# Memory attention and router of a hybrid decoder block: norms as numbers beside the products instead of rows ahead of them

## The reference, cut to what matters

```python
def rms_norm(x, g):                      # row by row, over the last axis
    return x * rsqrt(mean(x * x) + 1e-6) * g

# x: 256 tokens x 1024;  mem: 256 rows x 1024
x = x + parallel_head_groups(rms_norm(x, g_mix), ...)            # 16 heads, three kinds
q = rms_norm((rms_norm(x, g_xmem) @ w_mq).reshape(4 heads, 64), g_qm)
k, v = split(rms_norm(mem, g_mem) @ w_mkv);  k = rms_norm(k, g_km)
x = x + softmax(q @ k.T * 64 ** -0.5) @ v @ w_mo                 # memory attention
h = rms_norm(x, g_ffn)
logits = h @ w_router + b_router                                 # 32 experts, top 4
x = x + sum over experts of gate * (clamped_swiglu(h @ w_e1[e] + b_e1[e]) @ w_e2[e] + b_e2[e])
```

## Time and profile before

| | us |
|---|---|
| median of 3 runs | 1224.62 (1220.62 to 1225.78) |
| the profiled execution, its own time | 1226.69 |
| its span, first to last instruction | 1224.9 |
| TensorE busy | 1136.0 (93% of the span) |
| VectorE busy | 324.1 (26%) |
| ScalarE busy | 193.5 (16%) |
| GpSimd busy | 111.0 (9%) |
| mean granted TensorE clock | 0.965 of 2.4 GHz |

### The profile page before, as it was taken

The page is one execution under the profiler, slowest core; times in us unless marked ns, Lnnn a source line. Parts: engine busy times, 40 slices in busy tenths (PEclk is TensorE's granted clock), DMA queues, the critical chain, the costliest instruction groups (busy, mean ns, idle before and its releaser), DMA issues.

```text
span 1224.9 us, 13760 instructions
## 1 busy us (share of the span) xinstructions
PE 1136.0 (93%) x4992; PEld 459.6 (38%) x4992; DVE 324.1 (26%) x693; ACT 193.5 (16%) x391; POOL 111.0 (9%) x286
## 2 busy tenths in 40 slices
PE   6989978778999999999999999999999999999997
PEld 4656844653333333333333333333333333333332
DVE  4464644531121212111111112221111112111122
ACT  2133332211111111111111111111111111111111
POOL 1020100001001010000000000000111000001000
PEclk9979988677999999999999999999999999999999
DMA  7813335203999999999999999999999999999995
GB/s 259 319 35 138 134 102 194 102 1 135 403 430 429 429 429 429 428 429 429 428 428 428 428 428 428 428 428 428 428 430 429 428 429 430 430 428 429 428 429 238
DMA packets 44036, 430.54 MB, mean 351 GB/s; under 512 B 6289, under 2 KB 13713, under 8 KB 19185
## 3 DMA queue, kind: packets, MB, share of 16 engines
q1 hardware_dynamic: 43024, 427.67, 83.6%
q10 hardware_dynamic: 992, 2.62, 0.6%
HBM read 429.23 MB, written 1.05 MB: 351 GB/s over the span
## 4 chain that ended last, share of the span: by engine, by line
DMA 50%; PE 42%; DVE 4%; ACT 2%; issue 1%; SPq 0%; DVEq 0%; POOL 0%; ACTq 0%; POOLq 0%
DMA ring_w<-in_w_e_dram 49%; PE banks L580 12%; PE banks L267 11%; PE banks L561 8%; PE banks L593 3%; PE banks L255 2%; PE banks L509 1%; PE banks L302 1%; PE banks L536 1%; DMA w_in_cq<-in_w_in_dram 1%; PE banks L284 1%; PE banks L283 1%; PE banks L517 0%; PE banks L545 0%; DVE stat L1144 0%
## 5 line engine op out<-in xcount | busy, mean ns | idle before, releaser
L561 PE MATMUL banks<-ring,xg_T 128*64 128x512 f32 x2048 | 480.5, 601 | 27.2 <-DMA ring<-in_w_e_dram 25.3
L561 PEld LDWEIGHTS banks<-ring,xg_T 128*64 128x64 f32 x2048 | 134.3, 137 | 317.0 <-issue 239.8
L580 PE MATMUL banks<-ring_w,act_T 128*64 128x512 f32 x1024 | 237.8, 598 | 10.3 <-DMA ring_w<-in_w_e_dram 10.3
L1484 DVE TENSOR_TENSOR x_sb<-x_sb,banks 128x1024 f32<-128x1024 f32 x64 | 78.2, 1221 | 402.6 <-PE banks L536 386.0
L580 PEld LDWEIGHTS banks<-ring_w,act_T 128*64 128x64 f32 x1024 | 68.4, 136 | 150.7 <-issue 114.3
L1494 DVE TENSOR_TENSOR glu<-banks,b_T 128x512 f32<-128x512 f32 x32 | 22.1, 692 | 337.5 <-PE banks L593 337.5
L536 PE MATMUL banks<-y_sb,hot_gate_T 64*128 64x512 f32 x256 | 72.0, 640 | 1.7 <-ACT hot_gate_T L1071 1.7
L509 PE MATMUL banks<-h_sb,hot_slot 128*64 128x512 f32 x264 | 64.0, 607 | 2.5 <-POOL hot_slot L820 2.5
L1040 ACT COPY xg_rows<-banks 128x512 f32<-128x512 f32 x33 | 19.3, 586 | 294.0 <-PE banks L509 294.0
L1054 ACT COPY hidden<-banks 128x1024 f32<-128x1024 f32 x32 | 32.4, 1012 | 206.5 <-PE banks L561 206.5
L827 POOL COPY picked<-slot_table 128x2 f32 (+1 forms) x32 | 6.3, 196 | 579.2 <-PE banks L525 579.2
(11 more groups left out here) (257 smaller groups left out, 830.6 us busy)
## 6 DMA issues: line engine op xcount, KB each, us to landing
ring<-in_w_e_dram SPq DMA_DIRECT2D x128, 2048.0 KB, 23.8
ring_w<-in_w_e_dram SPq DMA_DIRECT2D x62, 2048.0 KB, 24.3
w_out_sb<-in_w_out_dram SPq DMA_DIRECT2D x1, 4096.0 KB, 13.4
ring_w<-in_w_e_dram SPq DMA_DIRECT2D x4, 1024.0 KB, 6.7
w_in_qk<-in_w_in_dram SPq DMA_DIRECT2D x1, 2048.0 KB, 14.3
w_mkv_sb<-in_w_mkv_dram SPq DMA_DIRECT2D x1, 2048.0 KB, 10.7
w_in_cq<-in_w_in_dram SPq DMA_DIRECT2D x1, 1536.0 KB, 11.7
w_in_qc<-in_w_in_dram SPq DMA_DIRECT2D x1, 1536.0 KB, 17.1
```

The source lines that it names most:

```text
L561: ins = TE.matmul(PS[SLOTS * h:SLOTS * h + SLOTS, B_W1 + b, :], left, ring1[:, u, 2 * F * j + F * h + 512 * b:2 * F * j + F * h + 512 * b ...
L580: ins = TE.matmul(PS[SLOTS * h:SLOTS * h + SLOTS, B_W2, :], actT[:, c % 4, c // 4, :], ring2[:, k, D * j + 512 * h:D * j + 512 * h + 512], ...
L1484: V.tensor_tensor(X[:, t, :], X[:, t, :], PS[:, first:first + 2, :].rearrange("p b n -> p (b n)"), ALU.add).then_inc(S("added"), 1)
```

## The change

It covers the stage between the last output projection and the first gather.

- Raw rows of `X` are transposed, not normalized ones. The gain vectors of the two norms are multiplied into the weights instead: `g_xmem` into `w_mq`, `g_ffn` into `w_router`, by GpSimd, from columns `gcol` that ScalarE's queue loads (2 x 1024 single numbers, in the place of the broadcast of `g_xmem`). `g_qm` and the score scale go into the gain of the memory keys.
- The scale of a row of x1 drops out of the normalized query but for the epsilon, which VectorE corrects (`shift`). The scale of a query and head goes into the exponential as its per-row factor; its square sum comes from TensorE (`query_sums`, with the two columns `halves`). The scale of a row of x2 (`y2`) is multiplied to the router's logits and into the one-hot tile of each gather; GpSimd multiplies `X` by the gain `g_ffn` for the gather's rows.
- Queries leave their product already transposed (`queries`: the weights are the stationary side), and values too (`mem_values`). Attention goes by tile instead of by head; the probabilities are normalized before they are transposed.
- The order of all engines in the stage is new. The first one-hot tile is made by VectorE, directly from the ranks. Gates, counts, gate transposes and tables come later, beside or behind the first gather; `give_biases` follows chunks 0 and 2 of the first step instead of standing ahead of chunk 0 and behind chunk 1.

```diff
+        def turn_x(name, added_name, t):
+
             for half in range(2):
-                merge("wd", t, half, range(5, KC))
-
-        pe.wait_ge(S("w_mq_in"), 16)
-        for t in range(NT):
-            pe.wait_ge(S("x1_rows"), t + 1)
-            turn_rows("x1_", H, t)
-            pe.wait_ge(S("turned_out"), turn.n)
-            multiply(f"q{t}", rows(t), lambda c: wmq[:, c, :], KC)
-        for t in range(NT):
-            pe.wait_ge(S("mem_q_normed"), t + 1)
-            turn_blocks(f"q{t}", [qm[:, t, P * j:P * j + P] for j in range(2)])
-        pe.wait_ge(S("turned_out"), turn.n)
-        for what, h in order(MEM_H):
-            {"score": score, "turn": turn_p, "value": value}[what](f"x{h}")
-        pe.wait_ge(S("mem_attended"), 1)
-        turn_blocks("om", [om[:, t, P * j:P * j + P] for j in range(2) for t in range(NT)])
-        pe.wait_ge(S("turned_out"), turn.n)
-        pe.wait_ge(S("w_mo_in"), 16)
-        for t in range(NT):
+                pe.wait_ge(S("mm_out"), left_no[f"{added_name}{t}{half}"])
+                turn_blocks(f"{name}{t}{half}", [X[:, t, P * c:P * c + P] for c in range(4 * half, 4 * half + 4)])
...
+        def queries(t):
+
+            bank = into(f"q{t}", [("q_left", t + 1)])
+            for j in range(2):
+                for c in range(KC):
+                    if j == 0 and c % 4 == 0:
+                        pe.wait_ge(S("turned_out"), turned_no[f"x1_{t}{c // 4}"])
+                    ins = TE.matmul(bank[:, P * j:P * j + P], wmq[:, c, P * j:P * j + P], hT[:, c, t * P:(t + 1) * P],
+                                    start=(c == 0), stop=(c == KC - 1))
+            ins.then_inc(S("mm_done"), 1)
...
+            pe.wait_ge(S("q_squared"), t + 1)
+            bank = into(f"ss{t}")
+            for j in range(2):
+                ins = TE.matmul(bank[:, j:4:2], qsq[:, j, t * P:(t + 1) * P], halves, start=True, stop=True)
...
+            pe.wait_ge(S("q_left"), t + 1)
+            banks = [into(f"s{par}{t}", [("mem_exped", 4 * t + 2 * par + 2)]) for par in range(2)]
+            for j in range(2):
+                for par in range(2):
+                    r = 64 * par
+                    ins = TE.matmul(banks[par][:, T * j:T * j + T], qmT[r:r + 64, j, t * P:(t + 1) * P],
+                                    memT[r:r + 64, j, :], start=True, stop=True)
...
+                pe.wait_ge(S("probs_normed"), 2 * t + par + 1)
+                turn_blocks(f"pm{t}{par}", [Pm[:, t, 512 * par + P * k:512 * par + P * k + P] for k in range(4)])
...
+            bank = into(f"o{t}")
+            for j in range(2):
+                for c in range(2):
+                    for par in range(2):
+                        a = 256 + 64 * (2 * j + par)
+                        b = 512 * par + 256 * j + P * c
+                        ins = TE.matmul(bank[64 * par:64 * par + 64, P * j:P * j + P], KVm[:, c, a:a + 64],
+                                        H[:, t, b:b + P], start=(c == 0), stop=(c == 1))
...
+        out_d(0, 0)
+        out_d(0, 1)
+        out_d(1, 0)
+        turn_x("x1_", "wd", 0)
+        out_d(1, 1)
+        pe.wait_ge(S("w_mq_scaled"), 1)
+        queries(0)
+        turn_x("x1_", "wd", 1)
+        query_sums(0)
+        mem_scores(0)
+        queries(1)
+        turn_probs(0)
+        query_sums(1)
+        mem_scores(1)
+        pe.wait_ge(S("w_mo_in"), 16)
+        mem_values(0)
+        mem_out(0)
+        turn_probs(1)
+        mem_values(1)
+        turn_x("x2_", "mo", 0)
+        mem_out(1)
+        pe.wait_ge(S("router_scaled"), 1)
+        route(0)
+        turn_x("x2_", "mo", 1)
+        route(1)
...
+        bank = into("ranks")
+        pe.wait_ge(S("mask_ready"), 1)
+        TE.matmul(bank[:, 0:E], U[:, 1, :], mask[:, 0, 0:E], start=True, stop=True)
+        TE.matmul(bank[:, E:2 * E], U[:, 2, :], mask[:, 0, 0:E], start=True, stop=False)
+        pe.wait_ge(S("mask_ready"), 2)
+        TE.matmul(bank[:, E:2 * E], U[:, 1, :], mask[:, 1, 0:E], start=False, stop=True).then_inc(S("mm_done"), 1)
...
+        def count():
+
+            TE.matmul(PS[:, B_HID + 1, 0:E], U[:, 2, :], mask[:, 0, 0:E], start=True, stop=False)
+            TE.matmul(PS[:, B_HID + 1, 0:E], U[:, 2, :], mask[:, 1, 0:E], start=False,
+                      stop=True).then_inc(S("counted"), 1)
+
+        def turn_gates():
+
+            pe.wait_ge(S("gate_ready"), 1)
+            for t in range(NT):
+                ins = TE.transpose(PS[0:E, B_HID, P * t:P * t + P], rt[:, 6, t, 0:E], ident[:])
+            ins.then_inc(S("gates_turned"), 1)
...
         gather(0)
         turn_gathered(0)
-        give_biases(0)
+        count()
+        turn_gates()
         for c in range(KC):
             multiply_w1(0, c)
-            if c == 1:
-                give_biases(1)
+            if c in (0, 2):
+                give_biases(c // 2)
...
+        pool.wait_ge(S("g_columns_in"), 32)
+        pool.wait_ge(S("w_mq_in"), 16)
+        G.tensor_tensor(wmq[:], wmq[:], gcol[:, 0, :].unsqueeze(2).to_broadcast([P, KC, 256]),
+                        ALU.mult).then_inc(S("w_mq_scaled"), 1)
+        pool.wait_ge(S("router_in"), 16)
+        G.tensor_tensor(router_w[:], router_w[:], gcol[:, 1, :].unsqueeze(2).to_broadcast([P, KC, E]),
+                        ALU.mult).then_inc(S("router_scaled"), 1)
...
+            pool.wait_ge(S("mm_out"), left_no[f"mo{t}1"])
+            G.tensor_tensor(H[:, t, :], X[:, t, :], gain[:, 0, :], ALU.mult).then_inc(S("rows_gained"), 1)
...
-        act.dma_start(gain[:, 1, :], g_xmem[0].partition_broadcast(P)).then_inc(S("g_xmem_in"), 16)
+        act.wait_ge(S("x_rows"), NT)
+        for k, g in ((0, g_xmem), (1, g_ffn)):
+            act.dma_start(gcol[:, k, :], g[0].rearrange("(c p) -> p c", p=P),
+                          allow_slow_non_contiguous=True).then_inc(S("g_columns_in"), 16)
...
+                    A.activation(Pm[:, t, 512 * par + T * j:512 * par + T * j + T],
+                                 bank_of(f"s{par}{t}")[:, T * j:T * j + T], ACT.Exp, bias=q_bias[:, k:k + 1],
+                                 scale=q_y[:, k:k + 1], accum_out=q_sum[:, k:k + 1]).then_inc(S("mem_exped"), 1)
...
+        act.wait_ge(S("mm_done"), made["wd01"])
+        turned_rows("x1_", 0)
+        square_row("x1_0", 0, "wd01")
+        query_squares(0)
+        act.wait_ge(S("mm_done"), made["wd11"])
+        turned_rows("x1_", 1)
+        square_row("x1_1", 1, "wd11")
+        mem_exps(0)
+        query_squares(1)
+        probs_leave(0)
+        mem_exps(1)
+        probs_leave(1)
+        act.wait_ge(S("mm_done"), made["q1"])
+        for t in range(NT):
+            square_row(f"x2_{t}", t, f"mo{t}1")
             turned_rows("x2_", t)
-
+        act.wait_ge(S("mm_done"), made["router1"])
+        leave("b1", b1T[:].rearrange("p e (h k) -> p k (e h)", h=2), 8, 512)
...
+        link(V.scalar_tensor_tensor(out=gk[:], in0=SG["g_km"], scalar=HD ** -0.5, in1=SG["g_qm"],
+                                    op0=ALU.mult, op1=ALU.mult))
...
+            V.tensor_scalar(q_v[:, a], b[:, 0:4], 1.0 / HD, x1_eps[:, t:t + 1], ALU.mult,
+                            ALU.add).then_inc(S("mm_out"), 1)
             after_leaving()
-            dve.sem_inc(S("mem_q_ready"), 1)
-            head_sums(f"q{t}", SCR[:, 256 * t:256 * t + 256].rearrange("p (h d) -> p h d", h=MEM_H),
-                      cols_of(0, f"q{t}"))
-            y = roots(f"q{t}", [(0, MEM_H, HD)])
-            q4 = qm[:, t, :].rearrange("p (h d) -> p h d", h=MEM_H)
-            link(V.tensor_tensor(q4, q4, y.unsqueeze(2).to_broadcast([P, MEM_H, HD]), ALU.mult))
-            V.tensor_tensor(q4, q4, SG["g_qm"].unsqueeze(1).to_broadcast([P, MEM_H, HD]),
-                            ALU.mult).then_inc(S("mem_q_normed"), 1)
-        for what, h in order(MEM_H):
-            if what == "score":
-                score(f"x{h}")
-            if what == "value":
-                value(f"x{h}")
-        after_leaving()
-        dve.sem_inc(S("mem_attended"), 1)
-        dve.wait_ge(S("g_ffn_in"), 16)
-        add_and_norm("x2_", "mo", 0, "x1_11", "x2_ready", "x2_rows")
+            newton(q_v[:, a], q_y[:, a], q_w[:, a])
...
+                ins = V.tensor_reduce(q_peak[:, k:k + 2], b, AX.X, ALU.max, negate=True)
+            link(ins)
+            a = slice(4 * t, 4 * t + 4)
+            V.tensor_tensor(q_bias[:, a], q_peak[:, a], q_y[:, a], ALU.mult).then_inc(S("probs_scaled"), 1)
...
+            V.scalar_tensor_tensor(out=L[:, t, 0:E], in0=take(f"router{t}")[:, 0:E], scalar=y2[t], in1=SG["b_router"],
+                                   op0=ALU.mult, op1=ALU.add).then_inc(S("mm_out"), 1)
+            after_leaving()
+            link(V.max(out=top[:, t, 0:8], in_=L[:, t, :]))
+            link(V.match_replace(out=rep[:, t, :], in_to_replace=top[:, t, 0:8], in_values=L[:, t, :], imm_value=-3e38))
+            V.tensor_tensor(mask[:, t, 0:E], L[:, t, 0:E], rep[:, t, 0:E], ALU.not_equal).then_inc(S("mask_ready"), 1)
...
+        shift(0)
```

(51 more changed lines are left out.)

244 lines of the change are left out of this document (120 added, 124 removed).

## The result

The changed kernel takes 1192.75 us (median of 4 runs, 1189.89 to 1197.16), the kernel before 1225.2 (4 runs): ratio 0.9745, 95% interval 0.9717 to 0.9772. The profiled execution took 1195.12, with a span of 1193.3.

What follows compares the result with a forecast made beforehand. Before the expert-weight stream starts at 294.40, a chain of short engine steps bounds; behind it, DMA, an unchanged 930.5 us. Gather 21.0 earlier less 1.3 added gives 19.7 off the 1224.62 median: 1205 us, range 1196 to 1213.

Steps and rivals of the forecast that it cites:

- The stage up to the gather: From the first `wd` product at 199.49 to the first gather: gather forecast at 259.0 instead of 280.02, 21.0 us earlier.
- I take the middle of 255.5 and 262.4: Time of the first gather, set between two step-by-step sums that differ in TensorE's clock: 259.0.
- The walk's first value, 255.5: Step-by-step sum to the first gather with router products at the low-clock price and TensorE otherwise dense: gather at 255.5.
- Behind the gather: From first gather to first freed slot: four count records and two gate transposes added, 1.3 us dearer; bias move changes nothing.
- Upstream: Everything up to the first `wd` product at 199.49: claimed unchanged but for small additions with slack.
- the second walk: Low clock from gaps near 223 and 230 into `mo0`: queries +3.0, scores/values +1, transposes +1, `mo0` +1.7; gather at 262.4.
- My price at full clock, 53.4 us: Same step-by-step sum to the first gather with the router at full clock too: gather at 252.9.
- the 1 us that I had named as a sign of being wrong: TensorE waiting on VectorE's queue order (`o0` copy behind maxima, `mo11` add behind roots) beyond the 1 us counted.
- Low clock throughout: Rival: clock stays low from queries to gather; gather at 274.3, only 5.7 us earlier, total 1220; chance 0.08.
- The gain given back: Rival: first expert steps free slots too slowly, the weight stream idles, total 1224.6; chance 0.03.
- Single numbers: Rival: single-number gain loads hold the queues and delay the memory load; 1244 at 0.44 us a piece; chance 0.03.
- GpSimd in VectorE's way: GpSimd's gain products might hold up VectorE, tile 1's roots starting 0.5 late; 3 us kept, range's end 1213.

Runs made afterwards that it cites:

- c1: Kernel before with TensorE's idle gaps filled by unread products, in the changed stage and upstream: 1203.32 us, ratio 0.9827.
- b2: Changed kernel with TensorE's idle gaps filled by unread products, in the changed stage and upstream: 1181.96 us, ratio 0.9664.
- a1: Kernel before run again with no edit, for a second trace: 1224.39 us, ratio 1.001.
- b4: Changed kernel with each of its two loads of 1024 single numbers issued four times: 1194.3 us, ratio 0.9757 to the kernel before.
- d1: b2 without its two filler products ahead of the first gather: 1182.73 us, ratio 0.9653 to the kernel before.
- c2: Changed kernel with GpSimd's product of rows and gain written twice for each tile: 1196.96 us, ratio 0.9771 to the kernel before.
- d2: c1 without its three filler products ahead of the first gather: 1202.03 us, ratio 0.9825 to the kernel before.
- b1: Kernel before with TensorE's idle gaps filled by unread products in the changed stage only: 1215.01 us, ratio 0.9921.
- a2: Changed kernel with the old order behind the router (counts, gates, tables before the first gather): 1200.67 us, ratio 0.9824 to the kernel before.
- a3: Changed kernel with normalized, gained rows transposed again and weights unscaled: 1205.06 us, ratio 0.9842 to the kernel before.

## Why the prediction was off

The direction, the new order of work and the path held; the size failed. The trace has 31.9 us where I forecast 19.7. The 12.2 between come from three places.

- **The stage up to the gather: 6.9.** Forecast 59.5 us behind the first `wd` product, measured 52.58. The step that failed is "I take the middle of 255.5 and 262.4". The clock did fall in a gap ahead of `mo0` (5.40 instead of 3.44), but was full again from 231 and in the first router product (1.87 where I had 3.62), and low from 243. The walk's first value, 255.5, had the router low and the rest full, the second had the queries to `mo0` low; averaging put 3.5 us on top of a walk that already had both router products at the low clock (3.6 each). The rest, some 3.4: the routers 1.7 and 0.8 cheaper, sizes 1.7 by the end of `mo1` (scores 1.13 for 1.84, values 1.09 for 2.0, query products 3.73 and 3.84 for 4.16, `mo0` against them), and 0.9 back, since transposes and copy ahead of the second router product took 2.4 for 1.9 and the choice to the gather 3.8 for 3.4.
- **Behind the gather: 2.7.** Forecast 1.3 dearer, measured 1.4 cheaper (12.95 for 14.38). The added counts and gate transposes are there (1.3 of TensorE), but the expert products that follow ran at full clock from 258 on. So did the bias group ahead of the slot (1.98 us, 3.78 before). I priced this part's work and left its clock as it was. The filled kernels show it apart: 9.7 us in c1, 10.0 in b2.
- **Upstream: 2.5.** Forecast 0; a1 shows that this belongs to no edit. It is the luck of the two traces; without it the miss is 9.7 us.

The middle was wrong by more than bad luck. In b4, whose stage has no edit, the clock fell one gap earlier than in after, before the scores, as the second walk had it (TensorE's rows of b4, then of d1):

```profile
223.53 2.08 PE L492 MATMUL banks<-mem_kT,mem_qT 64*128 64x256 f32 x8
...
228.04 6.31 PE L273 MATMUL banks<-w_mo_sb,mem_oT 128*128 128x512 f32 x8 [0.53 <-DVE mem_oT L1568]
```

```profile
219.02 3.70 PE L283 MATMUL banks<-w_mo_sb,mem_oT 128*128 128x512 f32 x8
```

Scores took 2.08 us for 1.13, `mo0` 6.31 for 5.40, and yet the gather lay 53.35 us behind the first `wd` product, 0.8 later than in after; the second walk had it 6.9 later than the first. (Its terms, 3.0, 1, 1 and 1.7, add up to 6.7.) The largest wasn't there: the query products (+3.0) ran at full clock in after, b4 and c2. And slower scores and values go into a wait: `mo0` begins when VectorE has copied `o0`, 29.3 us behind the first `wd` product in after, 29.5 in b4, and 29.3 in d1, where the gaps are filled.

So the failure is in the main the clock. Ahead of the gather I priced more low clock than came, and behind it I carried over before's 14.4 us with the low clock that was in them. Before's stage is 94.9 us and 79.6 with the gaps filled (d2): 15.3 us of it were low clock, at the least, since some 7 us at 1.2 GHz remain there, at the gather. After's is 65.5, and 61.0 filled (d1): 4.5. Of the 29.4 us that the stage gained, 18.6 are work and order and 10.8 are clock, to about a microsecond, since a stage varies that much by itself (b4). My price at full clock, 53.4 us from the first `wd` product to the gather, was too high by 1.9 in b2 (51.5), where fillers held the gather back by 2.1, and by 3.8 in d1 (49.6), where they did not. (From two router products at full clock I took off 2.6; at the measured 0.117 a record it is 3.5.)

What held: the time behind the first load did not change (930.8 for 930.5); the norm of x1 lies under the fourth `wd` product; tile 1's softmax lies under `mo0`, the roots of x2 tile 0 under `mo1` and the first router product; b1's transposes under the choice. The maxima took 0.65 each for 0.7. GpSimd multiplied w_mq in 3.61 us (at most 6.4 by the 0.60 of the earlier trace rows, where I had 6.3) by 142.6, long before 208. `more_known` was late for nobody. One wait was longer than I counted, and by more than the 1 us that I had named as a sign of being wrong: VectorE copied `o0` behind the roots and maxima of tile 1 and left TensorE idle for 2.26 us (0.7 in the walk). It cost clock as well: `mo0` took 5.40 us, 3.70 in d1.

The rivals. Low clock throughout: no, 1.00 in [199 to 222], with 32 narrow products in each query group. The rule that I put beside it (the Trainium skill, TensorE: Matmul & The Clock Gate, "Part 4: PE-mode transpose": transposes don't count as work for the clock) agrees with b1, where 14 us of transposes and thin products did not bring it back. c1 shows the other side: the same stretch ran at full clock throughout. The gain given back: no. Single numbers: their loads take time of the issuing queue (b4), but nothing waited there. The rule that the prediction named (the Trainium skill, DMA: Bandwidth & Descriptors, "Rules for kernel authors") makes a strided last dimension one descriptor per element. No row here shows descriptors, and b4's 9.24 us for three such loads and 2.29 for the next three give no one price. The 0.05 us a number that I took is not shown either; the two loads of after landed 8.2 and 9.2 us after issue. GpSimd in VectorE's way: I kept 3 us in the range for it; it is real, 1.77 us for a step of 0.19, and in after only 0.47 us of cover was left. The Trainium skill has this too (SBUF — State Buffer, "SBUF: two separate sides"): VectorE with two operands in SBUF and a GpSimd instruction that reads SBUF take turns for a whole instruction, and the rows of c2 agree.

What stays open: where exactly the clock falls differs from execution to execution (low at 189 to 197 in some traces of either kernel, in others not), and with it some 2 to 3 us; the price of GpSimd's product in after is known only to about a microsecond. The medians of a2 and a3 lie 3 to 4 us farther off than their stages; that this is the clock ahead of the stage is shown only for a3's trace.

## What to carry to other kernels

Before costing an edit in a stage of short steps, ask what the old stage loses to the low clock: an edit that packs TensorE's work denser can gain that too, here 10.8 us on top of 18.6. Gaps that can't be closed can be filled with products into a bank that is overwritten next, ahead of the wait. With fillers upstream too the changed kernel ran in 1182 instead of 1193 us; in the changed stage alone they shortened the stage by 3.9 us and the median not at all. A filler that outlasts its wait delays: the two ahead of the gather held it back by 2.1 us in b2. And a chain of small steps should not be priced as the middle of two clocks: price both ends, leave out what goes into a wait for another engine, and run the filled version to know which part is clock.

## What the runs showed of the hardware

- The same mixed stretch ran at either level of the clock: transposes and 64-column products 14 us at 0.53 in b1, TensorE busy throughout, and at 1.00 in c1, where four records of 384 columns stood in a gap that was 1.8 us in b1.
- Float32 products of 128 columns take 0.117 us a record at full clock (32 in 3.73), and score products over 64 rows, two side by side, 0.14 (8 in 1.13), 0.26 at the low one (8 in 2.08 in b4). Value products of 128 columns over two halves of the output rows took 0.068 a record (16 in 1.09), those of before, of 64 columns, 0.125 at full clock in c1 (16 in 2.00).
- Loads of 1024 single numbers landed 3 to 9 us after issue; one stood 0.4 to 1 us in the issuing queue, but in b4 three more behind it took 9.24 us and the next three 2.29.
- A VectorE step of 0.19 us with two tensor operands took 1.77 beside a GpSimd product of 2.35, until that one's end.
